# Table steps, row copies and first weights re-ordered in a transformer layer kernel

## What is computed

```python
h = layer_norm(x, ln_in_g, ln_in_b)
z = h @ w_in                                   # q, k, v, ssm_in, two gates
y_attn = chunk_attention(q, k, v, rel_bias)    # 8 heads of 128
y_ssm = gelu(s5_scan(ssm_in, ...)); y_ssm = y_ssm * sigmoid(y_ssm @ w_ssm_glu)
merged = sigmoid(g_attn) * (y_attn @ w_attn_up) + sigmoid(g_ssm) * (y_ssm @ w_ssm_up)
h = layer_norm(alpha * h + merged @ w_mix_out, ln1_g, ln1_b)
ple = rms_norm(p @ ple_w_in, ple_norm_g) * sigmoid(h @ ple_w_gate)
# PEER: 8 heads pick 16 of 128 x 128 experts per token by two half keys
u = u_table[experts]; act = gelu(einsum('btd,btrkd->btrk', h, u))
ffn = einsum('btrk,btrkd->btd', gates * act, v_table[experts])
out = layer_norm(alpha * h + ffn + ple, ln2_g, ln2_b)
```

## Time and profile before

| | us |
|---|---|
| median of 3 runs | 3967.8 (3966.8 to 3970.59) |
| the profiled execution, its own time | 3965.28 |
| its span in the trace | 3963.5 |
| TensorE busy | 3700.7 (93%) |
| VectorE busy | 2861.7 (72%) |
| ScalarE busy | 1140.4 (29%) |
| GpSimd busy | 2312.2 (58%) |
| DMA, mean over the span | 311 GB/s |

### The profile page before, as it was taken

The page is one execution under the profiler, slowest core; times in us unless marked ns, Lnnn a source line. Parts: engine busy times, 40 slices in busy tenths (PEclk is TensorE's granted clock), DMA queues, the critical chain, the costliest instruction groups (busy, mean ns, idle before and its releaser), DMA issues. The chain is left out here.

```text
span 3963.5 us, 49639 instructions
## 1 busy us (share of the span) xinstructions
PE 3700.7 (93%) x17969; PEld 3211.3 (81%) x17969; DVE 2861.7 (72%) x3863; ACT 1140.4 (29%) x1377; POOL 2312.2 (58%) x1290
## 2 busy tenths in 40 slices
PE   6999999999988999999999999999918999999998
PEld 5778888787767688879999999999817888888886
DVE  7666666667762445869778656666658999999998
ACT  3232322333211332223333222222202333333332
POOL 7334343344433234446666648888877888887870
PEclk9999999999999999999999999999959999999999
DMA  6888888887877586998998889999878999999994
GB/s 230 279 292 279 291 284 283 288 294 275 296 260 255 185 296 226 387 397 279 351 313 276 276 286 341 339 342 339 330 282 345 388 373 382 383 382 373 386 374 188
DMA packets 409612, 1231.15 MB, mean 311 GB/s; under 512 B 77561, under 2 KB 122633, under 8 KB 327977
## 3 DMA queue, kind: packets, MB, share of 16 engines
q1 hardware_dynamic: 261784, 770.07, 55.9%
q0 software_dynamic: 63488, 302.31, 20.2%
q10 hardware_dynamic: 84240, 157.63, 10.8%
HBM read 1020.65 MB, written 344.45 MB: 344 GB/s over the span
## 5 line engine op out<-in xcount | busy, mean ns | idle before, releaser
L767 POOL TENSOR_TENSOR wlo<-raw,whi 128x1024 fp32r<-128x1024 f32 x296 | 758.8, 2586 | 1075.2 <-ACT whi L1122 527.7
L1315 PE MATMUL bank<-h_hi,whi 128*128 128x384 f32 (+1 forms) x3312 | 1191.9, 360 | 41.6 <-DVE wlo L1642 37.2
L1317 PE MATMUL bank<-h_hi,wlo 128*128 128x384 f32 (+1 forms) x3312 | 1181.3, 357 | 0.0
L1316 PE MATMUL bank<-h_lo,whi 128*128 128x384 f32 (+1 forms) x3312 | 1180.5, 356 | 0.0
L1315 PEld LDWEIGHTS bank<-h_hi,whi 128*128 128x128 f32 x3312 | 625.4, 189 | 99.9 <-DVE wlo L1642 45.4
L1317 PEld LDWEIGHTS bank<-h_hi,wlo 128*128 128x128 f32 x3312 | 624.9, 189 | 50.2
L1316 PEld LDWEIGHTS bank<-h_lo,whi 128*128 128x128 f32 x3312 | 625.6, 189 | 47.9 <-issue 0.2
L1642 DVE TENSOR_TENSOR wlo<-raw,whi 128x2048 fp32r<-128x2048 f32 x240 | 549.3, 2289 | 142.0 <-ACT whi L1241 84.6
L1613 PE MATMUL bank<-whi,ew_hi 128*128 128x512 f32 x1408 | 550.1, 391 | 98.1 <-DVE ew_lo L1642 95.9
L834 POOL DMA_INDIRECT gates_d<-gate_all,place_u x336 | 496.0, 1476 | 148.3 <-issue 129.8
L1615 PE MATMUL bank<-whi,ew_lo 128*128 128x512 f32 x1408 | 548.8, 390 | 0.0
(11 more groups left out here) (302 smaller groups left out, 4713.4 us busy)
## 6 DMA issues: line engine op xcount, KB each, us to landing
raw<-in_weights SPq DMA_DIRECT2D x388, 1024.0 KB
v_rows_d<-in_weights ACTq DMA_DIRECT2D x96, 1024.0 KB
tin<-in_weights SPq DMA_DIRECT2D x162, 512.0 KB, 6.0
u_rows_d<-tout SPq DMA_DIRECT2D x324, 256.0 KB, 6.8
u_rows_d<-u_tout SPq DMA_DIRECT2D x188, 256.0 KB
v_rows_d<-in_weights SPq DMA_DIRECT2D x32, 1024.0 KB
gates_d<-zeros SPq DMA_DIRECT2D x32, 768.0 KB, 16.1
act_d<-act_o ACTq DMA_DIRECT2D x128, 192.0 KB
```

Source lines behind the costliest of these rows:

```text
L767: pool.tensor_tensor(wlo[slot][:, part], raw[slot][:, part], whi[slot][:, part].bitcast(F32), ALU.subtract).then_inc(lo_made, 1)
L1315: pe.matmul(bank, whi[slot][:, cols], rhs_hi(c), start=c == 0, stop=False)
L1316: pe.matmul(bank, whi[slot][:, cols], rhs_lo(c), start=False, stop=False)
L1317: last = pe.matmul(bank, wlo[slot][:, cols], rhs_hi(c), start=False, stop=c == DC - 1)
```

## The change

Eight edits, all of order or place:
1. `OUT_STEPS` 12 to 8: 77 table steps instead of 81; `TURN_U` turns 51 slabs in the expert loop instead of 47.
2. `table_step` issues the stores of slab x-1 first and the loads of slab x behind them. In the up- and output projection, steps take turns between two `tout` buffers (`turned_in`).
3. In the output projection SyncE makes no step behind the third wide load (so none between it and the input bias `b_ln_in`); `ln_g`, `ln_b` and the embedding's operands stand behind the 13th load, and VectorE turns 3, 3 and 2 slabs ahead of the first three column groups instead of 4 each.
4. In a head, slot 3 moves out of the scan to behind the first two `bias_and_max`, slot 4 to behind the last two.
5. Row copies: 16 by SyncE in the heads (two at b = 4), 8 in the GLU, 32 with the queries, 16 with the gates (one per block), 24 in expert slabs 0 to 11 (two each), 32 in slabs 12 to 75 (one per two slabs).
6. GpSimd issues 225 scatters first, then two per gather, so that they end at gather 80. It waits for both store counters.
7. `dot_slab(k) = 70 + 4k/9`: all 128 dots lie in the loop, the last behind slab 126. `load_aux` for the first pair moves up to slab 122, `first_weights(q)` into the loop behind slabs 124 to 127.
8. ScalarE's gelu of `act_p` and VectorE's product with the gates move into the first pair of the down-projection.

```diff
-UP_STEPS, OUT_STEPS = 16, 12
+UP_STEPS, OUT_STEPS = 16, 8
-FIRST_SCATTERS = 200
+AUX_FROM = N_U - 6
+FIRST_SCATTERS = 225
...
-    return min(TD * PICKS, FIRST_SCATTERS + (3 * k + 1) // 2)
+    return min(TD * PICKS, FIRST_SCATTERS + 2 * k)
...
-    return 67 + 4 * k // 7
+    return TURN_U.stop + 3 + 4 * k // 9
...
+    def turned_in(x):
+
+        q = x - HEAD_STEPS
+        return (0, x) if q < 0 else (1, q // 2) if q % 2 == 0 else (0, HEAD_STEPS + q // 2)
...
                 if x > 0:
                     sp.wait_ge(tr_made, 2 * x)
+                if x > 0:
+                    k = turned_in(x - 1)[0]
+                    store_rows(tout[k], step_slab(x - 1), tout_stored[k])
                 if x < STEPS:
                     for h in range(2):
                         sp.dma_start(tin[h][:, :], weights[AT_U + step_slab(x), :, HALF * h:HALF * (h + 1)]
                                      ).then_inc(tin_landed[h], 16)
-                if x > 0:
-                    store_rows(tout, step_slab(x - 1), tout_stored)
...
-                    if b % 2 == 1:
-                        lay_rows(sp, i, b // 2)
+                    if b == 4:
+                        for n in range(HEAD_LAYS * i, HEAD_LAYS * (i + 1)):
+                            lay_rows(sp, n // 4, n % 4)
...
             for i in range(3):
                 load_wide(AT_OUT, i)
-                table_step(HEAD_STEPS + UP_STEPS - 2 + i)
+                if i < 2:
+                    table_step(HEAD_STEPS + UP_STEPS - 2 + i)
...
-                for c in range(2):
-                    lay_rows(act, HEADS + N_GLU // 2 + N_Q // 2 - 1 + o // 2, 2 * (o % 2) + c)
+                lay_rows(act, GATE_LAYS_AT + o // 4, o % 4)
...
-            def turn_slab(x):
-
-                dve.wait_ge(tout_stored, 64 * x + 64)
+            def turn_slab(x, k=0, used=None):
+
+                if k == 0:
+                    dve.wait_ge(tout_stored[0], 64 * (x if used is None else used) + 64)
+                elif used > 0:
+                    dve.wait_ge(tout_stored[1], 64 * used)
...
-                    if k == 2:
-                        slot(3)
                     dve.drain()
...
                 bias_and_max(0)
                 bias_and_max(1)
+                slot(3)
                 divide(0)
                 divide(1)
-                slot(4)
                 bias_and_max(2)
                 bias_and_max(3)
+                slot(4)
                 divide(2)
                 divide(3)
...
                 while dots < PICKS and dot_slab(dots) <= e:
                     dot(dots)
                     dots += 1
+                if e >= N_U - 4:
+                    first_weights(e - N_U + 4)
+            dve.drain()
+            low_part(0, 0)
             for k in range(dots, PICKS):
                 dot(k)
-            dve.drain()
-            low_part(0, 0)
-            for q in range(4):
-                first_weights(q)
-            dve.wait_ge(acts_made, 1)
-            tt(act_p[:, :], act_p[:, :], gate_p, ALU.mult)
```

More of the change, by code:

```diff
@@ L587, in _ @@
             sp.dma_start(p_sb[:, :, :], p_t).then_inc(ple_landed, 16)
[L588 removed]
+            for i in range(N_OUT - 3, N_OUT):
                 load_wide(AT_OUT, i)
[L590 to L594 removed]
             for i in range(2):
@@ L1161, in _, with queries @@
             up_pair(DC // 2 - 1, True)
-            def queries(start, end, more=None, lays=True):
+            def queries(start, end, more=None):
                 with act.Fori(start, end) as j:
@@ L1248, in experts @@
                     if lays:
-                        lay_rows(act, j + SB - U_LAYS, s)
+                        for c in range(2):
+                            lay_rows(act, 2 * j + U_LAYS_AT + s // 2, 2 * (s % 2) + c)
+                    if spare is not None and s % 2 == 0:
+                        lay_rows(act, spare[0], spare[1] + s // 2)
                     act.wait_ge(blk_done, BLK_U + e + 1)
@@ L1264, in _ @@
                 experts(j, True)
-            with act.Fori(U_LAYS, SB) as j:
+            with act.Fori(0, U_SPARE) as j:
+                for z in range(2):
+                    experts(2 * j + U_LAYS + z, False, (j + U_SPARE_AT, 2 * z))
+            with act.Fori(U_LAYS + 2 * U_SPARE, SB) as j:
                 experts(j, False)
-            act.wait_ge(u_used, PICKS)
-            act.activation(act_p[:, :], act_p[:, :], ACT.Gelu_apprx_tanh).then_inc(acts_made, 1)
             def expert_pair(J, nxt, last):
@@ L1927, in _ @@
                     dve.drain()
-            with dve.Fori(0, DC // 2) as j:
+            for j in range(DC // 2):
                 for s in range(2):
```

83 lines of the change are left out of this document (48 added, 35 removed).

## The result

| | before | changed |
|---|---|---|
| median of 4 runs | 3967.3 us | 4052.8 us |
| lowest to highest | 3965.9 to 3970.6 | 4050.1 to 4066.2 |
| profiled execution, its span | 3965.3, 3963.5 | 4050.1, 4048.2 |

The ratio is 1.022, with a 95% interval of 1.0197 to 1.0245. The forecast was 3914 (3870 to 3954). The time lies above the end of the range, and even above the rival that ended slower (4036).

A forecast was written before the change was run, and what follows sets the result against it. TensorE, busy for 93% of the span, was taken as the bound, so only its idle and half-clock time could be won. Terms -10 - 14 - 26 - 7 - 3 + 6 = -54 took 3967.8 us to 3914, range 3870 to 3954.

The forecast's parts named there:

- Term 1: Mixer heads: taking a table step out of the scan shortens each head; -10 us, from -22 to a loss of 10.
- The loop 58.8 + 4p: Mixer heads: time of one head, p being the table-step period; 104.0 us at the p of 11.3 taken.
- Wrong: ... heads over 106 us: Mixer heads: a head lasting over 106 us was named as a sign that the prediction is wrong.
- Term 2: Up-projection: with two tout buffers VectorE waits for the load alone; -14 us, between -3 and -23.
- Term 3: Output projection: earlier input bias and loads remove two idle pieces of TensorE; -26 us, -34 at best.
- Term 4: Gates: one row copy per block instead of two takes the transfers off the path; -7 us (-4 to -8).
- Term 5: First experts: moving row copies away wins back part of a 7 us saturation loss; -3 us, from -7 to +8.
- the rival that the copies only change place: Expert slabs 0 to 11 saturate as the gates did: +8 instead of -3, 3925 us; chance 0.12.
- Term 6: Dots in the expert loop: 5.6 us each for 80, then 3.8 for 47; the 95.9 us wait is spread; +6 us.
- The dots hold TensorE: Expert loop: two-input VectorE instructions hold GpSimd for their whole 2.3 us, cycle 7.1; 4036 us, slower; chance 0.05.

The follow-up runs named there:

- experiment 6: The kernel before with only the row copies changed as in the change: 3950.9 us, ratio 0.9965.
- experiment 2: The changed kernel with slot 3 back in the scan and slot 4 back behind the second division, stores still first: 3993.5 us, ratio 1.0060.
- experiment 4: The changed kernel with slots 3 and 4 back and two loads ahead of four stores in every table step: 3970.4 us, ratio 0.9998.
- experiment 5: The changed kernel with the row copies put back as in the kernel before: 4057.3 us, ratio 1.0219.
- experiment 1: The changed kernel with two loads first, then four stores, in every table step, both tout buffers kept: 4027.7 us, ratio 1.0145.
- experiment 9: The changed kernel with 3 scatters for 2 gathers instead of 2 for 1, dots still dense: 4010.4 us, ratio 1.0110.

## Why the prediction was wrong, point by point

**Term 1, the heads: the step that failed is p,** the period of the table steps. The loop 58.8 + 4p came out right as a sum; for p I took 12.05, from the output projection, then 11.3. There are rows of the heads themselves, and they say otherwise: from slot 4 on 13.2, 15.0 and 12.1 us (the earlier trace rows and the two rows under experiment 6). In the changed kernel, the turns of one head, from slot 3 in its new place to `f_tab`:

```profile
557.87 2.37 DVE L1802 STREAM_TRANSPOSE tout<-tin 128x1024 f32<-128x1024 f32 x2
...
570.24 2.48 DVE L1802 STREAM_TRANSPOSE tout<-tin 128x1024 f32<-128x1024 f32 x2 [5.89 <-DMA tin<-in_weights]
...
583.62 2.52 DVE L1802 STREAM_TRANSPOSE tout<-tin 128x1024 f32<-128x1024 f32 x2 [9.72 <-DMA tin<-in_weights]
...
597.33 2.56 DVE L1802 STREAM_TRANSPOSE tout<-tin 128x1024 f32<-128x1024 f32 x2 [11.18 <-DMA tin<-in_weights]
...
609.90 2.37 DVE L1802 STREAM_TRANSPOSE tout<-tin 128x1024 f32<-128x1024 f32 x2 [0.29 <-issue]
...
615.99 0.76 DVE L160 SCALAR_TENSOR_TENSOR f_tab<-t,t 128x576 f32<-128x576 f32 x1
```

Four steps take 52.0 us, p = 13.0, and 58.8 + 52 = 110.8; this head lasts 110.7 (505.27 to 615.99). Over all seven a head lasts 108.8, which makes p 12.5. At the 11.3 that I took it was to be 104.0.

That 58.8 fits so well is luck. From slot 0's end to `f_tab` this head takes 4.5 us and not 8.6, and from the end of `f_tab` to the scan 20.9 (506.03 to 526.97) and not 16.9: the loop let the scan start when h_st is filled, and the turn of slot 2 stands ahead of it. It did in the kernel before as well. In the changed one it waits for its load:

```profile
524.36 2.53 DVE L1802 STREAM_TRANSPOSE tout<-tin 128x1024 f32<-128x1024 f32 x2 [8.92 <-DMA tin<-in_weights]
```

A step in the scan covers a whole period of transfers at 2.4 us of VectorE. Taking slots 3 and 4 from their places costs 53 us over the heads by experiment 2 (837.5 against 784.2). The loop did count that period, but at the price of a calmer stage, and so a loss looked like a gain of 10. "Wrong: ... heads over 106 us" stood in the prediction as the sign.

**And a gain I had not seen.** The half of the row copies that leave the heads, "which helps" in my words, gave 18 to 28 us at the last `f_tab` (experiments 6, 4 and 2); with the slots where the change put them it is 9 (experiment 5, 846.2 for 837.5). It got no number of its own.

**Term 2, the up-projection: the step "with two it waits for the load alone" failed, since it took no account of when the load is issued.** With the stores first, both loads wait for SyncE's 3 us of issue, and VectorE waits 7.68 us for them (experiment 1). The forecast -14 was +3.5. The second `tout` is worth 24 us against the kernel before (174.5 for 198.1), but only with the loads first (experiment 1). I had counted the megabytes in the queue and not the time that SyncE needs to issue them, which is in the trace.

**Term 3, the output projection, was right**: -30.6 for -26, and the wait at the fifth wide block is gone. With the loads first, all 42 us go (experiment 1). **Term 4, the gates, was right**: -7.7 for -7.

**Term 5, the first experts:** for -3, nothing. The 9000th weight load of TensorE, behind these copies, stands at 2019.3 for 2019.2, where the gates had ended 1.1 us later. The slabs that have fewer copies now did gain, but TensorE stood once for 7.3 us in the slabs that have more. The kernel before does not have this wait, and the one with the copies alone does (7.1 us). Between 1763 and 2020 us of the changed kernel:

```profile
PE bank L1341 <- POOL wlo L788: 7.3, 1, 7.3
```

So the rival that the copies only change place was partly right there. And the copies from slab 12 on, which the prediction had "under" the limit at 325 GB/s, cost 16 to 18 us up to the first dot: from 2184 to 2267 us, at a DMA share of 0.93 and 316 GB/s, a store that VectorE waits for is already late.

**Term 6, the dots, failed by 73 us, in three steps.** The first dot: 2375.8 for 2356.5, by the late copies (18 us beyond the 1.1 that the kernel is late at the end of the gates). Then the pace while scatters last, 5.6 us per dot; dot 80 is here:

```profile
2843.71 2.29 DVE L2203 SCALAR_TENSOR_TENSOR u_row<-u_row,h_tok 128x2048 f32<-128x2048 f32 x1 [1.05 <-DMA u_row<-u_rows_d,expert_u]
```

that is 467.9 us for 80 dots, 5.85 each, 28 us more than reckoned. GpSimd's groups from 2380 to 2830 us:

```profile
L855 POOL DMA_INDIRECT gates_d<-gate_all,place_u x152 | 250.4, 1647 | 74.8 <-issue 71.2 <-DMA gates_d<-gate_all,place_u 3.6
...
L864 POOL DMA_INDIRECT u_row<-u_rows_d,expert_u x76 | 109.5, 1440 | 23.2 <-issue 23.2
```

The excess over 0.96 us is 141 us, for 77 dots and 34 low parts: 1.27 us each, the 1.25 of the prediction. What was short is the pause between instructions, 98.0 / 228 = 0.43 us for 0.30; three of them a cycle make 0.4 us, which is all of the 0.25 that was missing and a little more. And the last 47 dots took 206.8 us, 4.4 each for 3.8: I had let the gathers run alone, but each is 1 MB, and 2.25 of them per slab share the transfers with its weights; the DMA share is 0.97 there. That the full transfers set this pace is argued from that share, not shown by a run of its own.

But the larger error lies ahead of these numbers. I took the new order of GpSimd's work as given and only added it up. Two scatters per gather keep it too slow for 2.25 dots a slab in the first stretch and leave it idle in the second, and experiment 9 gets 42 us back with that one number.

**The rivals.** "The dots hold TensorE" (0.05) had the right sign and the right place, but not its price: the cycle is 5.9 us and not 7.1, since each of VectorE's two-input instructions prolongs GpSimd's by 1.27 us in the mean, not by its whole 2.3. The rule of the Trainium skill named there (GPSIMD Engine Reference, section 8, Key points), that the two engines contend, agrees with the trace in kind; its price had to come from the rows. The fault of 45 us in the heads had no rival though rows of the heads stood against it, and the only one for the dots, off by 73 us, was put at a cycle that the rows already spoke against. So 0.89 for faster was far too sure.

## What to carry to other kernels

A step that looks like a cost in a critical stretch may cover a whole period of a chain of transfers: before moving it, count the periods that then stand one behind the other, with the period read in that stage and not in a calmer one. When a second buffer takes a wait off the path, issue what is now waited for first, and count the issue time of the queue. A helper engine that is nearly the bottleneck wants an even load: here, work put ahead of schedule slowed the first stretch, and the second could not give it back. And a hole of one engine is free time only if the engine that must fill it has room later.

## What the hardware showed that I had not expected

VectorE is held as well, not only GpSimd. Two instructions of one scan in the kernel before, a shade apart in size:

```profile
518.45 0.75 DVE L1642 TENSOR_TENSOR t<-t,t 128x248 f32<-128x248 f32 x2
...
521.32 4.97 DVE L1642 TENSOR_TENSOR t<-t,t 128x240 f32<-128x240 f32 x2
```

A pair that takes 0.75 us elsewhere takes 4.97, 4.2 us more, and others in that scan 2.0 to 2.6 more. GpSimd's row at that time, two low parts of a slab, each with two inputs:

```profile
520.81 5.21 POOL L767 TENSOR_TENSOR wlo<-raw,whi 128x1024 fp32r<-128x1024 f32 x2 [5.90 <-ACT whi L973]
```

VectorE's slow pair begins 0.5 us behind GpSimd's and ends 0.3 us behind it (526.29 and 526.02). The other slow ones of that scan, from 511.55 and from 533.20 on, also lie at GpSimd's low parts (509.70 to 514.91, 533.32 to 538.29). That these are what holds VectorE is read from the rows alone, since no run here took them away. It fits that from slot 3 to slot 4, with the same instructions between them, it is 19.1 us in the kernel before (526.94 to 546.07) and 16.4 in most heads of experiment 2, where the low parts fall at other instructions.
